# Loads of x and context moved from GpSimd's queue to the sync engine's, and the forget gates taken out first

## The reference, cut to what matters

```python
# first network, each layer; z is the context stream
mx = split(silu(c) @ w_mod[l] + b_mod[l], 9); mz = split(silu(c_ctx) @ w_mod[l] + b_mod[l], 9)
x = x + 0.5 * mx[2] * swiglu(rms_norm(x) * (1 + mx[1]) + mx[0], ffn1_w1[l], ffn1_w3[l], ffn1_w2[l])
...
# second network, each layer: 16 meta tokens ahead of the 256, L = 272
xn = rmsnorm(h, attn_norm_g)
fq, fk, fv, flog, rq, rk, rv, rg = split(xn @ w_in)
logf = log_sigmoid(flog + b_fgate)           # forget gates: 8 heads
c = cumsum(logf, axis=1)
s = q @ k.T * scale + c[t] - c[s]            # causal softmax of s, times v: 4 pairs of heads
# retention: rotated rq, rk with a fixed decay, group norm, times silu(rg)
h = h + concat(fox, ret) @ w_out
h = h + swiglu(rmsnorm(h, ffn_norm_g), w_gate, w_up, w_down)
```

## Time and profile before

| what | value |
|---|---|
| three timed runs | 2406.01, 2408.04, 2409.37 us |
| profiled execution, its own time | 2407.92 us |
| its span in the trace | 2405.7 us |
| TensorE busy | 2364.2 us (98%) |
| VectorE busy | 1536.9 us (64%) |
| ScalarE busy | 1013.0 us (42%) |
| GpSimd busy | 400.7 us (17%) |
| mean granted clock of TensorE | 0.996 |
| DMA, mean over the span | 150 GB/s |

### The profile page before, as it was taken

How to read it: one execution, slowest core, us unless ns; L and a number is a source line. 1 busy time by engine, 2 the same in 40 slices (tenths; PEclk the granted TensorE clock), 3 DMA queues, 4 the chain that set the end, 5 groups by cost and what they waited for, 6 DMA issues and landing times.

```text
span 2405.7 us, 36502 instructions
## 1 busy us (share of the span) xinstructions
PE 2364.2 (98%) x14394; PEld 2047.7 (85%) x14394; DVE 1536.9 (64%) x2617; ACT 1013.0 (42%) x1690; POOL 400.7 (17%) x425
## 2 busy tenths in 40 slices
PE   9999999999999999999999999999999999999998
PEld 6888888777888888888888877999888999899887
DVE  5888765874799855523323585666666665667874
ACT  5222234654522222422223465545345444446663
POOL 2221211340222221111011130121000220000110
PEclk9999999999999999999999999999999999999999
DMA  9566542112366754222222222555433555434554
GB/s 350 193 209 210 179 154 90 62 54 97 126 212 242 242 207 158 88 97 97 96 97 97 90 71 91 183 184 186 150 106 132 176 174 176 144 115 153 189 190 134
DMA packets 97864, 360.75 MB, mean 150 GB/s; under 512 B 11024, under 2 KB 11792, under 8 KB 96544
## 3 DMA queue, kind: packets, MB, share of 16 engines
q1 hardware_dynamic: 75744, 272.84, 33.8%
q0 software_dynamic: 21952, 85.59, 10.0%
HBM read 357.34 MB, written 1.05 MB: 149 GB/s over the span
## 4 chain that ended last, share of the span: by engine, by line
PE 90%; DVE 3%; ACT 3%; issue 2%; DMA 1%; POOL 0%; DVEq 0%; ACTq 0%; POOLq 0%
PE bank L810 25%; PE bank L811 24%; PE bank L812 24%; PE bank L817 6%; PE bank L818 3%; ACT ring_high L1382 1%; PE bank L1162 1%; PE bank L1150 1%; PE bank L1132 1%; DVE ring_low L1883 1%; PE bank L1184 1%; DMA arena<-w_mod_first_dram 1%; PE bank L1111 0%; PE bank L1331 0%; DVE arena L1949 0%
## 5 line engine op out<-in xcount | busy, mean ns | idle before, releaser
L1883 DVE TENSOR_TENSOR ring_low<-ring,ring_high 128x1024 fp32r<-128x1024 f32 x520 | 639.0, 1229 | 508.6 <-ACT ring_high L1382 506.4
L810 PE MATMUL bank<-x_parts,ring_high 128*128 128x512 f32 (+2 forms) x2308 | 802.7, 348 | 6.7 <-DVE x_parts L1958 3.7
L1382 ACT ACTIVATE ring_high<-ring 128x1024 fp32r<-128x1024 f32 x520 | 547.9, 1054 | 585.6 <-PE bank L812 544.7
L812 PE MATMUL bank<-x_parts,ring_low 128*128 128x512 f32 (+2 forms) x2308 | 788.9, 342 | 0.0
L811 PE MATMUL bank<-x_parts,ring_high 128*128 128x512 f32 (+2 forms) x2308 | 787.5, 341 | 0.0
L810 PEld LDWEIGHTS bank<-x_parts,ring_high 128*128 128x128 f32 x2308 | 437.4, 190 | 73.9 <-issue 14.2
L812 PEld LDWEIGHTS bank<-x_parts,ring_low 128*128 128x128 f32 x2308 | 437.3, 189 | 47.6
L811 PEld LDWEIGHTS bank<-x_parts,ring_high 128*128 128x128 f32 x2308 | 437.8, 190 | 46.6 <-issue 1.0
L642 POOL TENSOR_TENSOR hidden_parts<-fresh,hidden_parts 128x512 fp32r<-128x512 f32 (+2 forms) x132 | 203.6, 1542 | 1010.6 <-ACT hidden_parts L1515 1010.6
L1896 DVE CUSTOM_DVE_ANT_0 mod_products<-mod_ring,csilu 128x1024 bf16<-128x1024 f32 x224 | 303.1, 1389 | 32.0 <-DMA mod_ring<-w_mod_dram 30.8
L810 PE MATMUL bank<-hidden_parts,ring_high 128*128 128x512 f32 (+2 forms) x814 | 280.9, 345 | 0.2 <-POOL hidden_parts L642 0.2
(11 more groups left out here) (267 smaller groups left out, 2754.8 us busy)
## 6 DMA issues: line engine op xcount, KB each, us to landing
ring<-stream_dram SPq DMA_DIRECT2D x517, 512.0 KB, 3.3
mod_ring<-w_mod_dram POOLq DMA_DIRECT2D x128, 512.0 KB, 4.5
arena<-w_mod_first_dram POOLq DMA_DIRECT2D x8, 1024.0 KB, 11.8
ring<-stream_dram POOLq DMA_DIRECT2D x3, 512.0 KB, 10.7
arena<-na_bias_dram POOLq DMA_DIRECT2D x2, 768.0 KB, 12.1
mod_ring<-consts_dram POOLq DMA_DIRECT2D x1, 1076.0 KB, 5.4
resid<-x_dram POOLq DMA_DIRECT2D x2, 512.0 KB, 5.9
resid<-ctx_dram POOLq DMA_DIRECT2D x2, 512.0 KB, 7.1
```

The source lines that it names most:

```text
L810: pe.matmul(out, w[0][:, b], xh, start=start, stop=False)
L812: return pe.matmul(out, w[1][:, b], xh, start=False, stop=stop)
L1382: act.activation(high[:, i % SPLIT], ring[:, u % LOADED], ACT.Copy).then_inc(high_parts, 1)
L1883: dve.tensor_tensor(low[:, u % LOADED], ring[:, u % LOADED], high_f[:, i % SPLIT], ALU.subtract).then_inc(low_parts, 1)
```

## The change

x and context are loaded by SP's queue: x ahead of the condition columns and constants, context behind them, and the small vectors last. POOL's queue begins with piece 0. In `second_mixing`, DVE takes FLOG out ahead of FK0, and PE, DVE and ACT do the first part of the forget gates in the step of FLOG itself, and DVE the second part in the step behind it.

```diff
         @block.sync
+            half = KC // 2
+            for i in range(2):
+                sp.dma_start(resid[:, i * half:(i + 1) * half, META:META + NX], A["x"][:, i * half:(i + 1) * half]).then_inc(
+                    *made(f"x_loaded{i}", i, by=16))
             sp.dma_start(c_cols, A["c_cols"].rearrange("p (c s) -> p c s", c=KC)).then_inc(
                 *made("c_cols_loaded", 0, by=16))
             sp.dma_start(const[:, 0:C_ONES64], A["consts"][:, 0:C_ONES64]).then_inc(*made("consts_loaded", 0, by=16))
+            for i in range(2):
+                sp.dma_start(resid[:, i * half:(i + 1) * half, META + NX:META + N1],
+                             A["ctx"][:, i * half:(i + 1) * half]).then_inc(*made(f"ctx_loaded{i}", i, by=16))
             sp.dma_start(small, A["small"]).then_inc(*made("small_loaded", 0, by=16))
...
-            half = KC // 2
-            for i in range(2):
-                pool.dma_start(resid[:, i * half:(i + 1) * half, META:META + NX], A["x"][:, i * half:(i + 1) * half]).then_inc(
-                    *made(f"x_loaded{i}", i, by=16))
-            for i in range(2):
-                pool.dma_start(resid[:, i * half:(i + 1) * half, META + NX:META + N1],
-                               A["ctx"][:, i * half:(i + 1) * half]).then_inc(*made(f"ctx_loaded{i}", i, by=16))
...
# second_mixing, on PE and on ACT
-                    if k == SLOT2[FLOG] + 1:
+                    if k == SLOT2[FLOG]:
...
# project, on DVE
-                        if i == 0:
+                        if dst == FLOG:
                             dve.wait_ge(*when("rstd", (("ffn", 0) if tag[1] else ("ffn2", 1), 0)))
...
# forget_gates, on DVE
-                if k == SLOT2[FLOG] + 1:
+                if k == SLOT2[FLOG]:
...
-                if k == SLOT2[FLOG] + 2:
+                if k == SLOT2[FLOG] + 1:
...
# second_mixing, on DVE
-                    if k < len(PROJ2):
+                    if k == 0:
+                        project(tp, PROJ2, SLOT2[FLOG], N2, proj2, VTEMP2)
+                    if k < len(PROJ2) and k != SLOT2[FLOG]:
                         project(tp, PROJ2, k, N2, proj2, VTEMP2)
```

## The result

The changed kernel takes 2417.41 us (median of 7 runs, 2415.28 to 2418.19), the kernel before, timed beside it, 2408.04 (7 runs). The ratio is 1.0037, 95% interval 1.0026 to 1.0047: **9.4 us slower**, outside the forecast's range (2402.0 to 2413.0) and on the other side of zero. The profiled execution took 2415.57 us with a span of 2413.5, against 2405.7 before: +7.8. It lies 1.8 us under its kernel's median, so the trace shows somewhat less than the 9.4.

A forecast was written before the change was run, and what follows sets the result against it. The prediction took the kernel to be bound by TensorE's chain of matmuls, which holds 90% of it. From 2407.9 us, -3.8 for the forget gates and +2.8 for the opening gave 2406.9 us, range 2402.0 to 2413.0.

The forecast's parts named there:

- Rival 5: Opening: x moves in 1 KB runs, each taking a turn against 8 KB rows; +17.4 us, 2421.5 us; chance 0.09.
- q0's joining: Opening: POOL's queue starts only after x and the condition columns have gone alone on SP's queue, at 4.5 us.
- Rival 2: Opening: POOL's queue joins at once, row by row, at 3.5 us; +7.3 us, 2411.4 us; chance 0.19.
- Rival 3: Opening: SP's queue is served first, so piece 1 lands at 17.6; -1.1 us, 2403.0 us; chance 0.18.
- Rival 1: Opening: DMA engines drain one whole load before turning to the other queue; +5.5 us, 2409.6 us; chance 0.15.
- From the landing to the first product: Opening: context's landing to its sum 3.5 us, then 5.8 from the mean to the first weight product.
- the opening's term: Opening: context lands at 15.0, first weight product at 24.3 instead of 21.46; +2.8 us, ends -1.1 and +17.4.
- The forget gates' term: Both mixings: TensorE's wait at L1300 goes; gain 1.7 us in the first, 2.1 in the second; ends 1.7 and 8.6.
- the lower end's mechanism: First mixing: the later wait for DVE's decay grows to about 2.3 us; slow clock behind it could take back 1.7.
- V's first turn: First mixing, behind the forget gates: TensorE was expected to wait about 1 us there for DVE's projection.
- Rival 4: Mixings: DVE is no bound behind the forget gates; gain 8.6 us, 2402.1 us; chance 0.06.
- The sum: Whole kernel: 2407.9 - 3.8 (forget gates) + 2.8 (opening) = 2406.9 us.

The follow-up runs named there:

- e_flat: Changed kernel, but each of SP's four loads of x and context writes one contiguous run of 4224 B a partition (result not the reference's); 2410.74 us, ratio 1.0015.
- e_cols_x_sp: Changed forget gates; SP: c_cols, x, constants, small; POOL: context, then pieces; against the kernel before: 2406.06 us, ratio 0.9995.
- the first kernel of part 2: Changed kernel with context's two loads back on POOL's queue ahead of the pieces, x still first on SP; 2408.41 us, ratio 1.0006.
- the gates alone: Kernel before with only the forget gates' change, loads as before; 2404.77 us, ratio 0.9991.
- e_fill: The gates alone plus six idle products on PE in the wait before each layer's first retention values; 2407.83 us, ratio 1.0002.
- e_opening_only: Kernel before with only the opening's change: x and context on SP's queue, old forget gates; 2420.37 us, ratio 1.0054.
- e_pool_waits: Changed kernel, but POOL waits for context's second load before issuing its first modulation piece; 2407.41 us, ratio 1.0002.
- e_rows: Kernel before with changed gates, early decay, and meta, x and context as one input in four 4224 B-a-partition loads on SP behind c_cols, no POOL wait; 2405.79 us.
- e_x0_sp: Kernel before with changed gates, early decay, and x's first half on SP behind c_cols, second half and context on POOL; 2402.07 us, ratio 0.9976.

## Why the prediction was wrong

**The step that failed** is in the opening: "Each of 16 engines moves 8 rows of a load", with x's rows of 4 KB taking 0.17 us. It took the packets of SP's queue to be those of POOL's, 96 for 0.35 MB. In these runs SP's queue hands over a packet for each run that is contiguous on both sides (370 packets for 0.37 MB here, 90 for 0.31 MB in e_flat); `resid` has 256 columns of x, then 256 of context for each chunk, so the runs are 1 KB. It put context's landing at 15.0 and the first weight product at 24.3; they came at 24.15 and 33.19. The constants and context needed 8 + 64 = 72 turns of each engine in place of 24, and c_cols 8 more. The page's count shows it:

```profile
DMA packets 99400, 360.75 MB, mean 149 GB/s; under 512 B 11024, under 2 KB 13840, under 8 KB 98080
```

Under 2 KB there were 11792 before; the 2048 more are the four loads at 512 runs of 1 KB each.

**Rival 5 was the right mechanism**, with 0.09. It gave 29.6 for the landing, 5.4 too late, by a size: it priced a turn of 1 KB at 0.08 us. The 370 packets of 1 KB that 16 engines moved in 1 us make it 0.043, and q0 joined at 5.2 us, not at 3.5. By then 915 of x's 1024 packets had started, which leaves each engine about 7 turns of x and the 80 behind them. The rest is 14.1 us for POOL's 56 rows, as in the rival, and 87 x 0.043 = 3.7 for q1's: 5.2 + 14.1 + 3.7 + 0.5 = 23.5, where the row shows 24.15. What spoke against the rival was evidence from the other queue, and the text itself said that of SP's queue with such a target no row told. That was a reason for a larger chance, not for 0.09.

**q0's joining.** The time nearly held: q0's first packet came at 5.2 us, when x was nearly through, and not at 3.5. The reason, that what q1 had handed over goes first, did not: in e_cols_x_sp q0 joined in 4.5-5, with less than half of x's packets moved. So this part was luck. Rival 2 is out. Rival 3, SP first, is out by the equal counts. Rival 1, whole loads in turn, is out by the changed kernel's counts: each engine has 32 packets of a half of context against 8 rows of a piece, so whole loads would go 4 to 1, and they go 100 to 100.

**The Trainium skill's rule** of the same section as in rival 1 ("DMA: Bandwidth & Descriptors", Queues, rings and completion order) is that an engine drains a packet of about 9 to 17 descriptors before it switches. If each run of 1 KB is a descriptor, that is 9 to 17 KB a turn for SP's queue, an estimate from the page's figure. This case's trace does not agree: the two queues' counts stay within 4 of each other through 941 packets.

**From the landing to the first product** I had 3.5 + 5.8 = 9.3 us; it was 9.0. Right.

**What the opening's term missed besides:** c_cols and the constants lost their place at the head of SP's queue. In the first kernel of part 2 ACT is held until 8.48, TensorE stands for 5.5 us and the first product comes at 25.19, 3.7 us late, which is more than my whole term of 2.8; c_cols ahead of x takes 2.0 of it back. I had them only in "the condition columns go alone", through at 4.5; they landed at 9.97. In the changed kernel this hides behind context.

**The forget gates' term, -3.8 us, was about right.** The cuts give -1.0 and -2.1 in the changed kernel (forecast -1.7 and -2.1), -0.9 and -2.85 alone, and -1.3 and -2.1 in the mean of the traces; the medians of the gates alone, -2.2 us, leave room for 0 to -4.3. In the first mixing the wait at L1331 was 2.19 us long (the text had "about 2.3"), and the lower end's mechanism, a slow clock behind it, took its part: 0.9 us by e_fill, not 1.7. That it was the gates that made this wait long is not shown, since it was 1.91 us with the old gates in e_opening_only. V's first turn waited 0.87 us (forecast about 1). Rival 4 is out.

**The sum**: -3.8 + 2.8 became -3.1 + 11.7, with -0.7 to -0.8 in stretches that neither edit touches.

## What to carry to other kernels

SP's and POOL's queue, both full, share by turns, not by bytes, so the one with the short packets starves. Before moving a load beside another, count its packets. On SP's queue they were the runs contiguous at both ends; POOL's queue moved the same load in packets of 4 KB, so the count has to be read anew for the queue that the load goes to. A load that the start waits for should have the engines to itself, by its place in a queue or by one wait of the other issuer, and the tiny loads that an in-order engine waits for go ahead of it. And where one wait of a chain is taken away, look at every later wait on the same engine's line, and add them up, before pricing the gain.

## What the runs showed of the hardware that I had not expected

- A queue's 64 B to 520 B rows take as many turns as long ones: c_cols, 8 KB, landed at 9.97 behind x and beside POOL's rows, and at 6.45 behind x with POOL waiting (e_pool_waits); first in its queue (e_cols_x_sp) it was in before 2.79.
- The first packet of POOL's queue comes at very different times. Issued at 1.25 to 1.27 us, it came in 3.5-4 us in the kernel before and in e_rows, in 4.5-5 or 5-5.5 with all of x on SP (e_opening_only, e_cols_x_sp; the changed kernel), in 5.5-6 in e_x0_sp; issued at 10.38, with SP's queue empty, in 11.5-12. What sets these delays is open, since packets of 4.2 KB on SP went with 3.5-4 once and with 5-5.5 once.
- Where TensorE had stood for 4.5 us (e_flat) and for 11.0 us (the changed kernel), the granted clock was 0.50, the lower level of 1.2 GHz, in 15-20, and the first products behind it took about twice as long (2.07 us for four idle products at 20.30, against 1.10 at 24.27). A wait of 2.19 us was followed by a window at 0.66 in the changed kernel; one of 2.72 us in e_pool_waits (12.57) was not followed by any window under 1.00.
